# A hybrid decoder layer on one core: the FFN's gate/up projection with two seven-product sets a column block

## The reference

```
x = x + merged @ w_out                       # x2 in the kernel
h = rms_norm(x, ffn_norm_w)
a = silu(h @ w_ffn_gate) * (h @ w_ffn_up)    # (256, 2048) @ (2048, 5632), twice
x = x + a @ w_ffn_down                       # (256, 5632) @ (5632, 2048)
```

## Time and profile before

| what | value |
|---|---|
| median of three runs | 2068.26 us |
| profiled execution, span of the core | 2065.0 us |
| TensorE busy | 2058.4 us |
| VectorE busy | 1531.8 us |
| ScalarE busy | 1126.8 us |
| GpSimd busy | 158.5 us |
| moved by DMA | 399.77 MB, 194 GB/s |
| gate/up part | 1350.9 to 1827.7 us |
| down projection | 1827.7 us to the end |

### The profile page before, as it was taken

One profiled execution on the slowest core, in us unless ns is written; L12 is line 12 of the kernel. 1 busy time (PEld: TensorE's weight loads), 2 busy tenths in 40 slices (PEclk: granted clock), 3 DMA queues, 4 the chain that ended last, 5 costly groups with the idle time before them and its releaser, 6 DMA issues.

```text
span 2065.0 us, 28156 instructions
## 1 busy us (share of the span) xinstructions
PE 2058.4 (100%) x9584; PEld 1698.2 (82%) x9584; DVE 1531.8 (74%) x1859; ACT 1126.8 (55%) x1441; POOL 158.5 (8%) x195
## 2 busy tenths in 40 slices
PE   9999999999999999999999999999999999999999
PEld 8888877778888888888888888888888888888887
DVE  6777866665757777777667887897777777787866
ACT  5444555555556666666655454555555555555553
POOL 1121000000012222222000000000000000000000
PEclk9999999999999999999999999999999999999999
DMA  7656675564565655656565647666766767656574
GB/s 247 199 179 204 194 214 169 167 174 142 184 204 185 183 183 183 183 183 183 172 192 185 211 162 239 192 205 205 213 193 198 219 205 215 196 184 219 181 241 156
DMA packets 209802, 399.77 MB, mean 194 GB/s; under 512 B 15873, under 2 KB 21426, under 8 KB 209730
## 3 DMA queue, kind: packets, MB, share of 16 engines
q1 hardware_dynamic: 205346, 384.79, 59.6%
q0 software_dynamic: 3776, 13.70, 2.6%
q10 hardware_dynamic: 608, 0.34, 0.1%
HBM read 387.18 MB, written 2.16 MB: 189 GB/s over the span
## 4 chain that ended last, share of the span: by engine, by line
PE 96%; DMA 2%; DVE 2%; ACT 0%; issue 0%; SPq 0%; DVEq 0%; POOL 0%; ACTq 0%; POOLq 0%
PE acc L2041 79%; PE side L2128 6%; PE acc L2128 4%; PE side L2057 3%; PE side L2341 1%; DMA w_raw<-in_w_ffn_down 1%; DVE w_lo L1833 1%; PE side L2196 1%; DVE w_raw L1754 0%; DMA x_row<-in_x 0%; PE side L2347 0%; PE acc L2057 0%; PE side L2270 0%; DMA w_raw<-in_w_ffn_up 0%; ACT w_hi L1034 0%
## 5 line engine op out<-in xcount | busy, mean ns | idle before, releaser
L1075 DVE TENSOR_TENSOR w_lo<-w_raw,w_hi 128x1024 fp32r<-128x1024 f32 x332 | 416.1, 1268 | 251.7 <-ACT w_hi L576 250.4
L576 ACT ACTIVATE w_hi<-w_raw 128x1024 fp32r<-128x1024 f32 x332 | 347.9, 1057 | 372.5 <-PE acc L2041 319.4
L2041 PE MATMUL acc<-w_hi,h_hi 128*128 128x512 f32 x1248 | 498.5, 399 | 0.2
L2041 PE MATMUL acc<-w_hi,h_lo 128*128 128x512 f32 x1248 | 487.2, 390 | 0.0
L2041 PE MATMUL acc<-w_lo,h_hi 128*128 128x512 f32 x1248 | 486.0, 389 | 0.0
L984 ACT ACTIVATE w_hi<-w_raw 128x1024 fp32r<-128x1024 f32 x209 | 220.4, 1060 | 215.5 <-PE acc L2041 132.7
L1749 DVE TENSOR_TENSOR w_lo<-w_raw,w_hi 128x1024 fp32r<-128x1024 f32 x209 | 252.8, 1223 | 93.9 <-ACT w_hi L984 87.7
L2041 PEld LDWEIGHTS acc<-w_hi,h_hi 128*128 128x128 f32 x1248 | 234.5, 188 | 51.0 <-issue 5.6
L2041 PEld LDWEIGHTS acc<-w_hi,h_lo 128*128 128x128 f32 x1248 | 234.2, 188 | 50.2
L2041 PEld LDWEIGHTS acc<-w_lo,h_hi 128*128 128x128 f32 x1248 | 234.7, 188 | 48.1 <-issue 1.9
L2041 PE MATMUL acc<-w_hi,x2T_hi 128*128 128x512 f32 x528 | 207.3, 393 | 0.1
(11 more groups left out here) (435 smaller groups left out, 3099.4 us busy)
## 6 DMA issues: line engine op xcount, KB each, us to landing
w_raw<-in_w_in SPq DMA_DIRECT2D x320, 512.0 KB, 4.3
w_raw<-in_w_ffn_gate SPq DMA_DIRECT2D x88, 512.0 KB, 4.3
w_raw<-in_w_ffn_up SPq DMA_DIRECT2D x88, 512.0 KB, 4.6
w_raw<-in_w_ffn_down SPq DMA_DIRECT2D x88, 512.0 KB, 4.7
w_raw<-in_w_ssm_proj SPq DMA_DIRECT2D x64, 512.0 KB, 4.6
w_raw<-in_w_attn_proj SPq DMA_DIRECT2D x32, 512.0 KB, 3.7
w_raw<-in_w_out SPq DMA_DIRECT2D x32, 512.0 KB, 5.0
acs_b<-acs_scratch POOLq DMA_DIRECT2D x16, 512.0 KB, 6.9
```

Of the source, the lines that this page charges most:

```text
L576: nc.scalar.activation(w_hi[:, r], w_raw[:, n % RING], ACT.Copy).then_inc(hi_ready, 1)
L1075: nc.vector.tensor_tensor(w_lo[:, r], w_raw[:, n % RING], w_hi[:, r].bitcast(F32), ALU.subtract).then_inc(lo_ready, 1)
L2041: done = nc.tensor.matmul(acc[p][:, t], a[:, k0 + kk, cut], w[:, r, kk], start=first and kk == n == 0, stop=last and kk == UK - 1 and n == 2)
```

## The change

Sets 0 (A) and 1 (B) of each block now have seven products each, sets 2 and 3 stay plain. Only block 0 (the head) takes all four sets plain. The products P1, P5, P6, P7 of both sets for block i + 1 are accumulated in `side` during block i; P2, P3, P4 belong to the block itself. Their combination is written into the accumulators before the block starts: ScalarE writes P1 to `acc[0][:, 0]` and the negated combination to `acc[0][:, 1]`, VectorE writes P5 plus the combinations to `acc[1]`, and the matmuls add on top. SiLU and gating then read the accumulators directly.

A set's weight sums are made by VectorE from three extra buffers `side_raw[s]` (first gate piece, both up pieces) and the ring's second gate piece; the second up piece is loaded twice. The accumulating DMA and GpSimd's part in it go. The transposes use `side[2:4]`, so P1A, the first to write `side[:, 2]`, waits for `a_lo`. The buffers of set B, and its tables, lie where `x2` was: `x2` is written to a DRAM scratch in the head (`park`, two writes of 1 MB) and read back in four pieces during the down projection (`back`). Core of the diff:

```diff
-FFN_ORDER = (0, 2, 1, 3)
+FFN_HEAD = ("G0", "G1", "U0", "U1", "G2", "G3", "U2", "U3",
+            "g0", "P1A", "g1", "P5A", "g2", "P6A", "g3", "P7A", "u0", "P1B", "u1", "P6B", "u2", "P7B", "u3", "P5B")
+FFN_PAIR = ("P2A", "P2B", "g0", "P4A", "g1", "P1A", "P4B", "g2", "P5A", "P6A", "g3", "P7A",
+            "P3A", "u0", "P1B", "u1", "P6B", "P3B", "u2", "P7B", "u3", "P5B")
+FFN_TAIL = tuple(name for name in FFN_PAIR if name[:2] not in ("P1", "P5", "P6", "P7"))
...
@@ SyncE, head @@
+            sp.wait_ge(x2_ready, 4)
+            park(1)
+            remainder(FFN_HEAD, "U2")
+            ffn_ring(FFN_HEAD, "g2", 0)
+            ffn_side(0, 2, CW)
+            park(0)
...
@@ SyncE, each block @@
+                if not last:
+                    remainder(names, "P4A")
+                    ffn_side(0, 2, column + CW)
...
@@ SyncE, down projection @@
+                    if g == 0 and 1 <= position <= D // CW:
+                        if position == 1:
+                            sp.wait_ge(mm_done, tables_read)
+                        back(position - 1)
...
@@ ScalarE: what each operand's copy waits for @@
+                elif name[:2] == "P1":
+                    act.wait_ge(side_in["AB".index(name[2])][0], pairs.now() * 16 + 32)
+                elif name[:2] == "P5":
+                    act.wait_ge(t1_ready, sums.now(1 + "AB".index(name[2])))
+                elif name[:2] == "P6":
+                    act.wait_ge(t2_ready, sums.now(1 + "AB".index(name[2])))
...
@@ ScalarE, after the copy for the unit four ahead of the one named @@
+                    if head and at == 7:
+
+                        act.wait_ge(s_summed, 2)
+                        act.wait_ge(x2_out, 16 * D // CW + 2 * 16)
...
+                    if at == names.index("g3"):
...
+                        for t in range(TT):
+                            last = nc.scalar.activation(gate_f[:, t], acc[0][:, t], ACT.Silu, scale=x2_scale[:, t:t + 1])
...
+                    if "P1B" in names and at == names.index("P1B"):
...
+                        nc.scalar.activation(mids[:, 0], side[:, 2], ACT.Copy).then_inc(p1_ready, 1)
+                        act.wait_ge(gate_f_ready, pairs.now(1))
+                        nc.scalar.activation(acc[0][:, 0], side[:, 2], ACT.Copy).then_inc(acc00_seeded, 1)
+                    if "P7B" in names and at == names.index("u3"):
...
+                        nc.scalar.activation(acc[0][:, 1], mids[:, 1], ACT.Copy, scale=-1.0).then_inc(acc01_seeded, 1)
...
@@ VectorE, after the remainder for the unit four ahead @@
+                    if not head and at == 0:
...
+                        nc.vector.tensor_tensor(acc[1][:], side[:, 0].unsqueeze(1).broadcast_to([P, TT, CW]), mids[:],
+                                                ALU.add).then_inc(acc1_seeded, 1)
+                    if not head and at == names.index("g0"):
                         product_lo(i - 1)
+                    if sides and at == names.index("P1A") - LEAD:
+                        first_sum(0)
+                    if sides and at == names.index("P6A") - LEAD - 3:
+                        third_sum(0)
+                    if sides and at == names.index("P6A") - LEAD - 2:
+                        second_sum(0)
+                    if sides and at == names.index("P1B") - LEAD:
+                        first_sum(1)
+                        third_sum(1)
+                    if sides and at == names.index("P6B") - LEAD - 1:
+                        second_sum(1)
+                    if sides and at == names.index("P6B"):
...
+                        link(nc.vector.tensor_tensor(mids[:, 0], side[:, 1], mids[:, 0], ALU.subtract))
+                    if sides and at == len(names) - LEAD:
+                        fourth_sum(0)
+                    if sides and at == names.index("P7B"):
...
+                        nc.vector.tensor_tensor(mids[:, 1], mids[:, 0], side[:, 3], ALU.subtract).then_inc(mids_ready, 1)
+                    if sides and at == len(names) - LEAD + 1:
+                        fourth_sum(1)
+                    if at == names.index("u3"):
...
+                            last = nc.vector.scalar_tensor_tensor(out=gate_f[:, t], in0=acc[1][:, t], scalar=x2_scale[:, t:t + 1],
+                                                                  in1=gate_f[:, t], op0=ALU.mult, op1=ALU.mult)
...
@@ TensorE @@
+                    if name == "g0" and not head:
+                        pe.wait_ge(acc01_seeded, pairs.now())
+                    if name == "P1A" and not head:
+                        pe.wait_ge(a_lo_ready, pairs.now())
...
@@ GpSimd @@
-                pool.dma_start(w_raw[:, 1], w_raw[:, 2], accum_op=ALU.add).then_inc(third_summed, 16)
```

More of the change, by code:

```diff
@@ new lines, in _ @@
+            for n in range(8):
+                load((w_ffn_gate, w_ffn_up)[n // 2 % 2], UK * (n % 2 + 2 * (n // 4)), 0)
+            unit.n -= 8
+            remainder(FFN_HEAD, "G2")
+            ffn_ring(FFN_HEAD, "g0", 0)
+            ffn_side(0, 0, CW)
+            remainder(FFN_HEAD, "G3")
+            ffn_ring(FFN_HEAD, "g1", 0)
+            ffn_side(0, 1, CW)
+            sp.wait_ge(x2_ready, 4)
+            park(1)
+            remainder(FFN_HEAD, "U2")
+            ffn_ring(FFN_HEAD, "g2", 0)
@@ new lines, in _, with back @@
+            with repeat(sp, (FF // CW - 3) // 2, [(unit, 2 * len(FFN_PAIR)), (sums, 4)]) as i:
+                ffn_pair(FFN_PAIR, i * (2 * CW) + CW)
+                ffn_pair(FFN_PAIR, i * (2 * CW) + 2 * CW)
+            ffn_pair(FFN_PAIR, FF - 2 * CW, more=False)
+            ffn_pair(FFN_TAIL, FF - CW, more=False, last=True)
+            tables_read = unit.n - len(FFN_TAIL) + FFN_TAIL.index("P3B") + 1
+            def back(c):
+                part = slice(c * CW, (c + 1) * CW)
+                sp.dma_start(x2[:, :, part], x2_dram[:, part].rearrange("(t p) d -> p t d", p=P)).then_inc(x2_back, 16)
@@ L535, in _ @@
                             load(w_ffn_down, row, col)
[L536 removed]
+                        unit.n += len(PRODUCTS) - 4
                         unit.early = 1
@@ L959, in product_hi @@
                 act.wait_ge(a_T, i + 1)
-                nc.scalar.activation(a_hi[:, bass.ds(i * CT, CT)], side[:, 0:2].rearrange("p b (n t) -> p (b n) t", t=T),
+                nc.scalar.activation(a_hi[:, bass.ds(i * CT, CT)], side[:, 2:4].rearrange("p b (n t) -> p (b n) t", t=T),
                                      ACT.Copy).then_inc(a_hi_ready, 1)
[L963 to L975, removed]
-                    else:
[L977 to L985, removed]
@@ L1821, in _ @@
-            ffn_pair(0, True)
-            with repeat(dve, FF // CW - 1, [(unit, OPERANDS), (raw, RAWS), (own, 3)]) as i:
-                ffn_pair(i + 1, False)
+                    if head and at == 2:
+                        stationary_sums(0)
+                    if head and at == 5:
+                        stationary_lo(0)
+                    if head and at == 6:
+                        stationary_sums(1)
+                    if head and at == 9:
+                        stationary_lo(1)
@@ new lines, in ffn_pair @@
+                pairs.step()
+                sums.step(2)
+            raw, pairs, sums = Tally(), Tally(), Tally()
+            raw.n = unit.n - LEAD - unit.more
+            ffn_pair(FFN_HEAD, FFN_PAIR, 0, True)
+            with repeat(dve, (FF // CW - 3) // 2, [(unit, 2 * len(FFN_PAIR)), (own, 2), (pairs, 2), (sums, 4)]) as i:
+                ffn_pair(FFN_PAIR, FFN_PAIR, i * 2 + 1)
+                ffn_pair(FFN_PAIR, FFN_PAIR, i * 2 + 2)
+            ffn_pair(FFN_PAIR, FFN_TAIL, FF // CW - 2)
```

439 lines of the change are left out of this document (278 added, 161 removed).

## The result

| | kernel before | changed kernel |
|---|---|---|
| median | 2067.92 us (2065.65 to 2069.1, 4 runs) | 2077.06 us (2074.47 to 2078.0, 4 runs) |
| ratio | | 1.0044, 95% interval 1.003 to 1.0059 |
| profiled execution, span | 2065.0 us | 2076.3 us |
| gate/up part | 1350.9 to 1827.7: 476.8 us | 1357.4 to 1837.0: 479.6 us |
| down projection | 237.3 us | 239.3 us |

The changed kernel is 0.44% slower, 9.1 us. The forecast was no change, 2068.0, with 2058 to 2079 as its range; the time lies inside the range, and the slowdown wasn't forecast.

What follows compares the result with a forecast made beforehand. TensorE, busy for all of the span, was taken as the bound, with a closed loop eating the saved matmuls. Gate/up −1.8 and down projection +1.4 gave −0.4: 2067.9, rounded to 2068.0 us, range 2058 to 2079.

Steps and rivals of the forecast that it cites:

- Edits costed at nothing, and their cover: Weight loads, head transfers of x2, table sums and SyncE's waits: taken as 0 us, bounded by 0 and +6.
- rival 3: Head's DMA queue: ScalarE waits for the second write of x2, up to 8 us, middle 2073; chance 0.13.
- The loop (steps 1 to 6): Once a column block, TensorE, ScalarE and VectorE wait for each other: 43.05 us, 1.36 longer than TensorE's own 41.69.
- this sign: Whole kernel: TensorE's busy time was to fall by about 12 us.
- Unknown costs: Writes to PSUM before each block: VectorE's to acc[1] taken as 1.14 us, at most twice that; ScalarE's two 0.48 each.
- rival 2: VectorE's write of acc[1] to PSUM costs more than one to SBUF: 3.6 to 10.3 us, middle 2075; chance 0.17.
- Rival 4: VectorE's operations in the blocks take the full 1.22 us from start to start: 1.5 a block, 2081; chance 0.05.
- Rival 1: In the blocks a_lo is ready before P1A, so a block takes 41.7 us and the kernel 2055.8; chance 0.15.
- Around the span: The 3.3 us between the profiled span of 2065.0 and the median of 2068.26 were taken to stay.
- Down projection: Four 512 KB transfers bringing x2 back ahead of weight loads: +1.4 us, bounds 0 and 5.2.

## Why the prediction was wrong, point by point

**The failed step** is in "Edits costed at nothing, and their cover": the head at 0, bounded by 0 and +6. That paragraph walked the head's transfers, tables and ScalarE's copies, and passed over TensorE's own waits. One of them had moved: `acc_free[1]` from ahead of the third unit to ahead of the first. It is a wait that the change adds in a new place, and behind it in TensorE's queue stood two units that didn't need it. Its price, 5.05 us of gap and 2.3 of lower clock, is what makes the sign: without it the kernel is 0.12% over the kernel before (interval 0.03% to 0.22%), all but inside the bound of 0.2%. None of the four rivals held this mechanism; rival 3 named the head but another cause (its waits were absent).

**The loop (steps 1 to 6)** was right as a mechanism. ScalarE's timeline gives its corners in one block:

```profile
1532.94 1.06 ACT L1126 ACTIVATE w_hi<-side_raw 128x1024 fp32r<-128x1024 f32 x1 [3.93 <-DVE side_raw L1934]
1533.91 1.99 ACT L1126 ACTIVATE w_hi<-w_raw 128x1024 fp32r<-128x1024 f32 x2
1535.80 0.58 ACT L1171 ACTIVATE mids<-side 128x512 f32<-128x512 f32 x1
1536.28 0.59 ACT L1173 ACTIVATE acc<-side 128x512 f32<-128x512 f32 x1
```

and VectorE's and TensorE's timelines the others:

```profile
1526.94 1.23 DVE L1917 TENSOR_TENSOR w_lo<-side_raw,w_hi 128x1024 fp32r<-128x1024 f32 x1 [1.49 <-ACT w_hi L1126]
...
1531.61 1.22 DVE L1934 TENSOR_TENSOR side_raw<-side_raw,side_raw 128x1024 f32<-128x1024 f32 x1
...
1537.87 1.22 DVE L1917 TENSOR_TENSOR w_lo<-side_raw,w_hi 128x1024 fp32r<-128x1024 f32 x1 [0.33 <-ACT w_hi L1126]
...
1552.10 1.23 DVE L1969 TENSOR_TENSOR acc<-side,mids 128x1024 f32<-128x1024 f32 x1
1553.24 1.22 DVE L1917 TENSOR_TENSOR w_lo<-side_raw,w_hi 128x1024 fp32r<-128x1024 f32 x1
...
1556.64 1.22 DVE L1909 TENSOR_TENSOR a_lo<-side,a_hi 128x1024 f32 x1
```

```profile
1514.62 0.49 PE L2315 MATMUL side<-w_hi,x2T_hi 128*128 128x512 f32 x1 [1.01 <-DVE a_lo L1909]
...
1525.65 0.39 PE L2315 MATMUL side<-w_hi,s_hi 128*128 128x512 f32 x1
...
1557.99 0.49 PE L2315 MATMUL side<-w_hi,x2T_hi 128*128 128x512 f32 x1 [1.04 <-DVE a_lo L1909]
1558.32 0.40 PE L2315 MATMUL side<-w_lo,x2T_hi 128*128 128x512 f32 x1
```

| step | forecast | measured, one block |
|---|---|---|
| 1, TensorE from P1A to the end of g3 | 10.88 | 1525.65 − 1514.62 = 11.03 |
| 2, to VectorE through ScalarE | 1.29 | 1526.94 − 1525.65 = 1.29 |
| 3, VectorE to the second sum's landing | 5.94 | 1532.94 − 1526.94 = 6.00 |
| 4, ScalarE's six copies | 4.90 | 1537.87 − 1532.94 = 4.93 |
| 5, VectorE to `a_lo` | 18.66 | 1556.64 − 1537.87 = 18.77 |
| 6, `a_lo` to the matmul, restart | 1.38 | 1557.99 − 1556.64 = 1.35 |
| sum | 43.05 | 43.37 |

The restart, 0.33 − 0.23 = 0.10, lies in step 1 of the table's right column and in step 6 of the left. From 1427.95 to 1774.52 eight blocks took 43.32 each, 0.27 over the forecast; no term is off by more than 0.15. Nine blocks of 0.27 are 2.4 us, and with the 2.3 of the clock they make 4.7; the gate/up part (479.6) passed the 475.0 forecast by 4.6. The busy time of TensorE fell by 4.5 us and not 12, because what counts as busy grew too: 2.3 us of lower clock, and at each wait the last matmul ahead of it counts with its whole 0.39 us instead of the 0.23 to the next, and the first behind it takes 0.10 more. The waits make nine times 0.26, another 2.3; 1.8 more was busy outside the gate/up part, and 1.3 of the missing 7.7 isn't traced. This is worked out and wasn't tried; this sign was ill chosen, while the waits themselves came as forecast (nine, 9.2 us together).

**Unknown costs.** The seed's write to PSUM has this group (count, busy, mean ns, idle before) in the blocks of the changed kernel:

```profile
L1969 DVE TENSOR_TENSOR acc<-side,mids 128x1024 f32<-128x1024 f32 x9 | 11.0, 1226 | 0.0
```

1226 ns, against 1221 for sums in SBUF, and the operation after it starts 1.14 later (1552.10 to 1553.24): the value taken, and rival 2 is out. For VectorE reading PSUM, the Trainium skill, "VectorE: DVE Perf Modes", section on the TRN2 errata, has a table with 62 cycles more than for SBUF (120 against 58, at 0.96 GHz), by estimate 65 ns. Here `a_lo`, with one of its two operands in PSUM, took 1219 ns, no longer than the sums, so the measurement decides against it for this operation.

**Rival 4** (spacings of 1.22) is out: the four operations from 1552.10 to `a_lo` at 1556.64 take 4.54, 1.135 each. **Rival 1** (loop not closed) is out for the changed kernel by its nine waits; the loop cut by one operation shows what less of it gives. The closed block was 1.63 over TensorE's own 41.69, 14.7 us in nine blocks; 0.77 a block, 6.9 in all, stayed, and 7.9 were gained.

**Around the span.** The sum put 3.3 us between span and median down to time around the span that stays. The other executions on record show 1.6 there (2077.9 against 2076.3 for the changed kernel); the other 1.7 is variation between executions of the kernel before. It doesn't touch the forecast, since the sum comes back to the median either way.

**Down projection.** Forecast +1.4, found +2.0 in the profiled execution. The mechanism isn't shown: over all kernels this part took 236.7 to 240.5 us, in no order that follows the read-back's place, and moving it gained nothing twice. A kernel without these transfers wasn't tried, so what they cost stays open.

## What to carry to other kernels

When a change rewrites the order of an engine's work, list every wait of that engine before and after with the unit it stands ahead of: a wait hoisted over units that don't need it shows nowhere in a sum of durations, and here it cost 6 to 9 us, about what the best order of the same change won (7.9). On an engine that is 92% busy, a sum of its work says little about what one more operation costs. The closed loop, walked from row to row, said it to 0.3 us of 43 and told which place is free and which costs in full. Where such a loop is closed, first move out of it what may come later: one sum, exchanged with the operation that ends the loop, turned a kernel 0.1% slower than before into one 0.3% faster.

## What the runs showed of the hardware

An idle time of 5.05 us on TensorE was followed by 4.8 us at the lower clock, and one of 5.58 us by 5.7: the matmuls came 0.43 us apart instead of 0.23. Nine waits of up to 2.3 us, each about 42 us after the last, left the granted clock at 1.00 in the profiled execution of the kernel with the extra operation in the loop. The slowest of that kernel's other three (2083.68 us) lists 0.997, about what the two kernels with the long idle time list (0.998), and has no trace that shows where. After a wait, the second matmul comes 0.33 us behind the first, whether TensorE had stood for 2.17 us (the kernel with the extra operation in the loop, 1554.08 to 1554.41) or had been a mere 0.15 late (the changed kernel, 1448.65 to 1448.98). And a wait for a semaphore that another engine raises with an instruction of its own can stand in the views as "issue", with no releaser, in one kernel and with the line that raises it in another.
